# The second tile pair of a decoder layer's feed-forward: weights loaded and prepared during the output projection, two of its products issued during the layer norm, and a new product order for the first two pairs

## The reference, cut to what matters

```python
h = layer_norm(ALPHA * x + mix @ w_o, ln1_w, ln1_b)
ff_gate, ff_up = jnp.split(h @ w_ffn_in, 2, axis=-1)     # D_FF = 2816
y = layer_norm(ALPHA * h + (silu(ff_gate) * ff_up) @ w_ffn_out, ln2_w, ln2_b)
```

## Time and profile before

| | us |
|---|---|
| three runs | 1117.37, 1119.82, 1124.09 (median 1119.82) |
| profiled execution | 1119.33, of which span 1117.5 |
| PE busy | 1051.7 (94%) |
| DVE busy | 727.2 (65%) |
| ACT busy | 452.6 (41%) |
| output projection on PE, from | 630.6 us of the span |
| first feed-forward tile, from | 690.4 |
| pair products, from | 727.1 |

### The profile page before, as it was taken

How to read it: one execution, slowest core, us unless ns; L and a number is a source line. 1 busy time by engine, 2 the same in 40 slices (tenths; PEclk the granted TensorE clock), 3 DMA queues, 4 the chain that set the end, 5 groups by cost and what they waited for, 6 DMA issues and landing times.

```text
span 1117.5 us, 19631 instructions
## 1 busy us (share of the span) xinstructions
PE 1051.7 (94%) x7868; PEld 1015.2 (91%) x7868; DVE 727.2 (65%) x1112; ACT 452.6 (41%) x860; POOL 196.7 (18%) x258
## 2 busy tenths in 40 slices
PE   6799999998999998999999999879999999999994
PEld 5799888987999997888999998779999999999994
DVE  4832277335678989975656568798888887723346
ACT  3633355442254454422522245555545454511221
POOL 3512000011147564464000012000000000000004
PEclk9899899999999999999999999999999999999997
DMA  9346122124321221134223245122323232422432
GB/s 273 93 135 217 38 58 58 57 87 148 125 77 39 57 58 57 58 94 124 77 77 94 86 142 145 44 57 79 111 80 110 82 109 64 135 72 85 130 106 90
DMA packets 167512, 106.87 MB, mean 96 GB/s; under 512 B 12072, under 2 KB 161248, under 8 KB 167408
## 3 DMA queue, kind: packets, MB, share of 16 engines
q1 hardware_dynamic: 161584, 85.01, 26.5%
q0 software_dynamic: 5184, 18.26, 5.1%
q10 hardware_dynamic: 656, 2.36, 0.6%
HBM read 99.65 MB, written 6.95 MB: 95 GB/s over the span
## 4 chain that ended last, share of the span: by engine, by line
PE 77%; DVE 13%; issue 3%; ACT 3%; DMA 1%; POOL 1%; SPq 0%; DVEq 0%; ACTq 0%; POOLq 0%
PE bank L835 13%; PE bank L836 12%; PE bank L837 12%; PE bank L926 6%; PE bank L929 6%; PE bank L928 6%; PE bank L883 3%; PE bank L881 3%; PE bank L882 3%; PE bank L1088 2%; DMA w_raw<-in_w_mem_kv 1%; DVE decay_q L2071 1%; PE bank L1071 1%; ACT w_hi L1458 1%; DVE a_masked L2084 1%
## 5 line engine op out<-in xcount | busy, mean ns | idle before, releaser
L835 PE MATMUL bank<-x_lo,w_hi 128*128 128x288 f32 x864 | 266.1, 308 | 2.7 <-DVE x_lo L1981 1.9
L836 PE MATMUL bank<-x_hi,w_lo 128*128 128x288 f32 x864 | 255.9, 296 | 0.0
L837 PE MATMUL bank<-x_hi,w_hi 128*128 128x288 f32 x864 | 255.8, 296 | 0.0
L835 PEld LDWEIGHTS bank<-x_lo,w_hi 128*128 128x128 f32 x864 | 164.1, 190 | 10.1 <-issue 6.7
L836 PEld LDWEIGHTS bank<-x_hi,w_lo 128*128 128x128 f32 x864 | 164.0, 190 | 0.1
L837 PEld LDWEIGHTS bank<-x_hi,w_hi 128*128 128x128 f32 x864 | 163.5, 189 | 0.0
L750 DVE TENSOR_TENSOR w_lo<-w_raw,w_hi 128x1024 fp32r<-128x1024 f32 x66 | 81.9, 1245 | 67.0 <-ACT w_hi L1458 66.8
L1458 ACT ACTIVATE w_hi<-w_raw 128x1024 fp32r<-128x1024 f32 x88 | 92.3, 1054 | 58.2 <-PE bank L837 36.9
L926 PE MATMUL bank<-x_sum_lo,pair_hi 128*128 128x288 f32 x320 | 94.7, 296 | 6.3 <-DVE hidden L1860 2.6
L929 PE MATMUL bank<-x_sum_hi,pair_hi 128*128 128x288 f32 x320 | 94.3, 295 | 0.0
L750 DVE TENSOR_TENSOR w_lo_out<-w_raw_out,w_hi_out 128x1024 fp32r<-128x1024 f32 (+1 forms) x30 | 35.3, 1178 | 70.3 <-ACT w_hi_out L1458 70.2
(11 more groups left out here) (316 smaller groups left out, 2655.3 us busy)
## 6 DMA issues: line engine op xcount, KB each, us to landing
w_raw<-in_w_in SPq DMA_DIRECT2D x46, 512.0 KB, 3.9
up_weights<-in_w_ffn_in SPq DMA_DIRECT2D x20, 512.0 KB, 4.0
gate_weights<-in_w_ffn_in SPq DMA_DIRECT2D x20, 512.0 KB, 5.0
w_raw_out<-in_w_ffn_out SPq DMA_DIRECT2D x20, 512.0 KB, 3.6
w_raw<-in_w_o SPq DMA_DIRECT2D x14, 512.0 KB, 3.6
w_raw<-in_w_mem_kv SPq DMA_DIRECT2D x8, 512.0 KB, 5.1
mem_ring<-in_mem_k_s POOLq DMA_DIRECT2D x8, 512.0 KB, 5.1
mem_ring<-in_mem_v_s POOLq DMA_DIRECT2D x8, 512.0 KB, 4.3
```

The lines of the kernel that those rows point to most:

```text
L835: pe.matmul(bank[:, 0:n], wh, lo, start=(i == 0), stop=False)
L836: pe.matmul(bank[:, 0:n], wl, hi, start=False, stop=False)
L837: mm = pe.matmul(bank[:, 0:n], wh, hi, start=False, stop=(i == len(parts) - 1))
```

## The change

SP loads up and gate of the second pair (q = 1) before the third and the fifth unit of the output projection; for this the wait for `mix_split` moves there. The second pair's `combine`, `pair_hi` and most of its `pair_lo` are placed behind `o` steps of half 0; `pair_lo` A1 comes in the second layer norm and `pair_lo` S24 just before the pair phase. The first pair's `combine`, and `pair_hi` A0 and S1, move ahead of the second half's `var`. P1 and P2 of the second pair are issued between fg(1,0) and fg(0,1). `x_sums` 3 comes before 2, and the low parts become steps of their own (`x_low`). The remaining products of the first two pairs get the order P1, P2, P5, P3, P6, then P5 of the second pair, P7, P3 of the second, P4, P6 of the second, and their snaps, sums and silus the positions of `FIRST_BESIDE`. A one-column Ln (`ln_table`) is put on ACT ahead of the output projection and after fg(0,0).

```diff
 ]
+X_ORDER = (0, 1, 3, 2)
+FIRST_PRODUCTS = [{"P1": 0, "P2": 1, "P5": 2, "P3": 3, "P6": 4, "P7": 6, "P4": 8},
+                  {"P5": 5, "P3": 7, "P6": 9, "P7": 15, "P4": 17}]
+FIRST_BESIDE = [
+    {("snap", "s1"): 1.05, ("sum", "C11"): 2.1, ("pair_silu", 0): 2.5, ("snap", "s5"): 3.05, ("snap", "s2"): 5.02,
+     ("sum", "C12"): 5.4, ("pair_silu", 1): 5.75, ("sum", "C22"): 7.05, ("pair_hidden", 1): 7.4,
+     ("pair_hidden", 0): 9.05},
+    {("snap", "s1"): 3.2, ("sum", "C11"): 3.6, ("snap", "s5"): 6.05, ("pair_silu", 0): 9.4,
+     ("snap", "s2"): 10.02, ("sum", "C12"): 10.4, ("pair_silu", 1): 10.75},
+]
 EARLY_HI = range(FIRST_PAIR, FIRST_PAIR + 6)
...
     for q in range(PAIRS):
-        steps += [(7 * q + at, ("product", name, q)) for name, at in PRODUCT_AT.items()]
-        steps += [(7 * q + at, (what, which, q)) for at, what, which in BESIDE_AT
-                  if q or what not in ("pair_hi", "combine", "pair_lo")]
+        first = q < len(FIRST_PRODUCTS)
+        products = FIRST_PRODUCTS[q].items() if first else [(name, 7 * q + at) for name, at in PRODUCT_AT.items()]
+        steps += [(at, ("product", name, q)) for name, at in products]
+        for at, what, which in BESIDE_AT:
+            if first and what in ("pair_hi", "combine", "pair_lo"):
+                continue
+            moved = FIRST_BESIDE[q] if first else {}
+            steps.append((moved.get((what, which), 7 * q + at), (what, which, q)))
         if FIRST_PAIR + q in EARLY_HI:
...
     extras = {(KT - 3, 1): [("var", 1, 0)], (KT - 4, 1): [("norm", 1, 0)]}
+    beside_o = {
+        (2, 0): [("combine", "S1", 1)],
+        (3, 0): [("combine", "S3", 1), ("combine", "S2", 1), ("pair_hi", "S1", 1), ("pair_hi", "A0", 1)],
+        (4, 0): [("combine", "S4", 1), ("pair_lo", "S1", 1)],
+        (5, 0): [("pair_lo", "A0", 1), ("pair_hi", "S24", 1)],
+        (6, 0): [("pair_hi", "A1", 1)],
+    }
+    steps.append(("ln_table",))
     for c, half in halves_order(O_TAIL):
...
         pending.append(mean(1, O_TAIL, half, c))
+        steps += beside_o.get((c, half), [])
         if (c, half) == (KT - 1, 1):
...
     out(first[0])
+    steps.append(("ln_table",))
     summed()
-    steps.append(("center", 1, 1))
+    steps += [("center", 1, 1), ("pair_lo", "A1", 1), ("pair_hi", "A0", 0), ("combine", "S1", 0), ("combine", "S3", 0),
+              ("pair_hi", "S1", 0), ("combine", "S2", 0), ("combine", "S4", 0)]
     late = [out(first[1], late="all")]
...
     late.append(out(first[2], late="all"))
-    steps += [("x_sums", 0), ("combine", "S1", 0), ("combine", "S3", 0)]
+    steps += [("product", "P1", 1), ("product", "P2", 1)]
     out(first[3])
-    steps += late[0]
-    steps += [("x_sums", 1), ("combine", "S2", 0), ("pair_hi", "S1", 0)]
+    steps += late[0] + [("x_sums", 0), ("x_sums", 1), ("pair_hi", "S24", 0)]
     out(first[4])
-    steps += late[1]
-    steps += [("combine", "S4", 0), ("pair_hi", "A0", 0), ("x_sums", 2)]
+    steps += late[1] + [("x_low", 0), ("pair_lo", "A0", 0)]
     out(first[5])
-    steps += [("pair_hi", "S24", 0), ("pair_lo", "S1", 0), ("pair_lo", "A0", 0)]
+    steps += [("pair_lo", "S1", 0), ("pair_lo", "S24", 0), ("x_sums", 3)]
     for key in ffn_order(1):
         out(key)
-    steps += [("x_sums", 3), ("pair_lo", "S24", 0), ("pair_hi", "A1", 0), ("pair_lo", "A1", 0)]
+        steps += [("x_low", 1), ("pair_hi", "A1", 0)] if key[2] == 0 else []
+    steps += [("x_sums", 2), ("x_low", 2), ("pair_lo", "A1", 0), ("pair_lo", "S24", 1), ("x_low", 3)]
     steps += pair_steps()
...
         def _(sp):
+            w_ffn = a["w_ffn_in"].rearrange("(k p) n -> p k n", p=P)
+            o_unit = OUTS["o", 0, 0][0][0]
+            def load_up(q):
+                c0 = FF + (FIRST_PAIR + q) * P
+                if q >= 3:
+                    product_done(sp, "P4", q - 3)
+                sp.dma_start(A1[q % 3][:], w_ffn[:, :, c0:c0 + P]).then_inc(up_in[q % 3], 16)
+            def load_gate(q):
+                c0 = (FIRST_PAIR + q) * P
+                if q >= 2:
+                    product_done(sp, "P2", q - 2)
+                sp.dma_start(A0[q % 2][:], w_ffn[:, :, c0:c0 + P]).then_inc(gate_in[q % 2], 16)
             sp.dma_start(IDENT[:], a["c_ident"]).then_inc(ident_in, 16)
...
                     unit_used(sp, u - NRAW)
+                if u == o_unit + 2:
+                    sp.wait_ge(mix_split, 2 * KT)
+                    load_up(1)
+                elif u == o_unit + 4:
+                    load_gate(1)
                 for dst, src in unit_source(u):
                     sp.dma_start(dst, src).then_inc(raw_in[u % NRAW], 16)
-            w_ffn = a["w_ffn_in"].rearrange("(k p) n -> p k n", p=P)
-            sp.wait_ge(mix_split, 2 * KT)
             for q in range(PAIRS):
-                c0 = (FIRST_PAIR + q) * P
-                if q >= 3:
-                    product_done(sp, "P4", q - 3)
-                sp.dma_start(A1[q % 3][:], w_ffn[:, :, FF + c0:FF + c0 + P]).then_inc(up_in[q % 3], 16)
-                if q >= 2:
-                    product_done(sp, "P2", q - 2)
-                sp.dma_start(A0[q % 2][:], w_ffn[:, :, c0:c0 + P]).then_inc(gate_in[q % 2], 16)
+                if q != 1:
+                    load_up(q)
+                    load_gate(q)
             for u in range(UNIT2, len(UNITS)):
...
                     i = rest[0]
-                    act.wait_ge(x_sum, (1, 5, 9, 13)[i])
+                    act.wait_ge(x_sum, 4 * X_ORDER.index(i) + 1)
                     copy(TSH[:, i], TS[:, i]).then_inc(x_sum_hi, 1)
+                elif what == "ln_table":
+                    act.activation(LBT[:, 8:9], EPS[:, 0:1], ACT.Ln)
                 elif what == "pair_hi":
...
                     ins.then_inc(x_sum, 1)
-                for t in {1: (0,), 3: (1, 2, 3)}.get(i, ()):
-                    dve.wait_ge(x_sum_hi, t + 1)
-                    dve.wait_ge(x_sum, {0: 5, 1: 13, 2: 13, 3: 13}[t])
-                    dve.tensor_tensor(TSL[:, t], TS[:, t], f32(TSH[:, t]), ALU.subtract).then_inc(x_sum_lo, 1)
+            def x_low(t):
+                dve.wait_ge(x_sum_hi, X_ORDER.index(t) + 1)
+                dve.wait_ge(x_sum, {0: 5, 1: 9, 2: 13, 3: 9}[t])
+                dve.tensor_tensor(TSL[:, t], TS[:, t], f32(TSH[:, t]), ALU.subtract).then_inc(x_sum_lo, 1)
             def pair_combine(name, q):
...
                     x_sums(rest[0])
+                elif what == "x_low":
+                    x_low(rest[0])
                 elif what == "combine":
...
```

## The result

The changed kernel takes 1126.63 us (median of 8 runs, 1121.15 to 1129.13), the kernel before 1118.65 (8 runs). The ratio of the runs, which is not the quotient of the two medians, is 1.006, with a 95% interval of 1.0037 to 1.0084. So it is slower by 4 to 9 us, some 0.6%. The forecast was 1121.2, with 1125.5 as the range's upper end: the median lies 1.1 above that end, and 1.006 times 1118.65, which is 1125.4, just inside it. The profiled execution took 1127.08. Of the executions further down, one of e5 took 1820.70 at a granted clock of 0.714, where the other nine had 0.981 to 0.987, and is left out of its row.

What follows compares the result with a forecast made beforehand. PE was taken as full except for holes set by DVE, some 7.5 us at the entry to the pairs and 2 in the layer norm. 1119.33 + 2.35 (late load) - 0.5 (gain) = 1121.2 us; range 1112.5 to 1125.5.

Steps and rivals of the forecast that it cites:

- Cost 2.35: Output projection: unit 2 lands late behind the wait and up(1), so tile (2,0) starts at 642.5 instead of 640.15.
- the burst's second load: Earlier group of loads at 690.57, whose second landed 5.3 us after issue; used to time the projection's unit 2.
- kept open and taken as nothing: Half clock on PE after the 2.35 hole at tile (2,0): no loss charged, both ends kept.
- the rest of this preparation costs nothing: Output projection: sums and low parts added on DVE fit its free time; units 3 and 4 make no second hole.
- the row: Profile row for the second layer norm: Ln and Exp each had a 1.28 us load, so Exp's stays on the chain.
- that rival: Second layer norm: one table set holds exp and ln, so the norm ends 1.28 sooner, 1119.9 us; chance 0.05.
- The added Ln only moves a table load: Second layer norm on ACT: the early load delays the squares by 0.4, covered by the 16 var matmuls.
- walking DVE's list: Entry to pairs: 22.8 us of DVE work puts P3(0) at 735.5 after a 6.0 hole; 3.3 more before P5(2).
- the 1.4 charged: Entry to the pairs: half-clock loss on PE of 1.4 us after the 6.0 hole ahead of P3(0).
- the gain of 0.5: P5 of the third pair starts at 751.3 against 751.84, the layer norm's 3.18 included.
- reach C11 by the end of P5(0): Entry, first rival: DVE reaches C11(0) by 729, no hole at P3(0); 1113.8 or 1111.4 us; chance 0.18.
- The slower rival: Projection: loads ahead of units 2 and 4 land at 3.1 us intervals, half clock twice; 1127.7 us, chance 0.12.

Runs made afterwards that it cites:

- e5: Kernel before with only the wait for the mix's last low part put ahead of the projection's unit 2 load; 1118.40 us, ratio 0.9998.
- e1: Changed kernel with up(1) issued ahead of the projection's unit 4 and gate(1) ahead of unit 5; 1121.71 us, ratio 1.0023.
- e6: Changed kernel without the two one-column Lns on ACT; 1128.54 us, ratio 1.0081.
- e2: Changed kernel with the first pair's snap s5 ahead of its first silu on ACT; 1119.67 us, ratio 1.0005.
- e7: e3 with the third pair's four sums and S1's high and low parts ahead of the hidden product waiting for P4(0); 1112.99 us, ratio 0.9946.
- e4: Changed kernel with the second pair's P1 and P2 moved from the layer norm to between the first pair's P5 and P3; 1125.19 us, ratio 1.0042.
- e8: e7 with the second pair's P1 and P2 moved from the layer norm to between the first pair's P5 and P3; 1114.92 us, ratio 0.9971.
- e9: e7 with the low part of the third pair's A1 placed behind the second pair's C22 on DVE; 1113.48 us, ratio 0.9941.
- e3: Changed kernel with both later pair loads (ahead of units 4 and 5) and snap s5 ahead of the silu; 1117.29 us, ratio 0.9977.

## Why the prediction was right or wrong

**Loads beside the projection.** The mechanism was right, its size was not: this is the step that failed. "Cost 2.35" was 5.2. Tile (2,0) started 3.7 later from the projection's start than before, because unit 2 landed 6.8 after its issue, where the sum took the 5.3 of the burst's second load; why it was 6.8 is open. And half clock followed the hole, 1.5, which I had kept open and taken as nothing. That "the rest of this preparation costs nothing" held but for 0.9 at most (e1).

**The layer norm.** P1 and P2 filled it, and fg(0,1) ended when it did. The Exp load of 1.28 stayed behind the early Ln (709.49), as the row said. So the Trainium skill's one set for exp and ln ("ScalarE: Activation LUTs", "Table sets: the hidden batching unit") is not what this kernel gets, and that rival is out. "The added Ln only moves a table load" was wrong: it takes the load from behind `pair_hi` A0 and S1, which the change put ahead of Ln, and e6 has that at 1.1 us, of which about 0.5 would be left with gate(0) landing as in the changed kernel.

**The entry.** P3(0) was forecast by walking DVE's list: 11.2 us behind the end of fu(1,1) (735.5 against 724.3). It came 10.9 behind (742.46, 731.54), and for the reason given: from the end of the norm's last `x_lo` (718.2) to C11 (741.13) DVE took 22.9, where 23.1 was forecast (710.99 to 734.1). The hole was 5.61 for 6.0, the one ahead of P5(2) 3.21 for 3.3. e2 and e7 show that both are the orders named: the snap behind the silu, the sums behind the hidden product. The half clock behind the first lasted longer than the 1.4 charged: P3 and the three products behind it took 8.9 us instead of 6.4, 2.5. So the gain of 0.5 became a loss of 0.5. Of the 4.1 by which the stage is longer than forecast, 2.6 are half clock (1.5 and 1.1) and 1.4 the later landing.

**The rivals.** DVE did not reach C11 by the end of P5(0). The slower rival named late loads and half clock, at units 2 and 4; what happened was unit 2 alone, by both of its means. Its 0.12 was too little: three holes above 2.3 us each stood in my own sum, and for the clock behind them the sum took nothing twice and 1.4 once.

## What to carry to other kernels

Where two engines take their work from one ordered list, a copy that frees a bank should not stand behind an operation that waits for a third engine: here the order of two steps in a list was worth 6 us. Work put into a stall pays only if what comes behind it can start sooner, so walk the list of the engine that sets the next stage before counting a filled hole as gain. With a load of 512 KB slipped in front of it, and another right behind, a load that was needed soon landed 3 us later; with the two pair loads further down that stretch lost 0.9 at most.

## What the runs showed of the hardware that was not expected

The first norm's hole of 2.4 to 2.5 us is the same in all eleven profiles, and the tile behind it took 3.24 in five of them and 4.55 to 4.79 in six (before, changed, e2, e4, e8, e9). The hole of 3.21 ahead of P5 of the third pair is the same in six profiles: the clock stayed full behind it in three (changed, e1, e2) and fell to half in three (e3, e4, e6). PE behind it, the changed kernel and then e3:

```profile
760.00:762.00 2.00, 2.00 (x18) 1.00 0.00 1
```

```profile
750.00:752.00 2.00, 2.00 (x10) 0.50 0.00 0
```

One hole, one length, and the clock fell to half or stayed: a single profile is off by 1.5 us for this alone, and a change of that size in one can't be ascribed to an edit. The hole at tile (2,0) (3.6 to 4.5 us, four profiles) and that of 5.6 ahead of P3 (three) were followed by half clock each time, and the price was no fixed one: in the changed kernel 1.5 us behind the first and 2.5 behind the second.
